# Four modulation loads issued ahead of the small vectors' wait, and TensorE's own quarter moved behind VectorE's three

## The reference

```python
def first_block(x, c, w_ada, b_ada, norm1_w, w_in, ...):
    c_act = jax.nn.silu(c)
    for l in range(DEPTH):                       # DEPTH = 1
        mod = c_act @ w_ada[l] + b_ada[l]        # (1, 1024) @ (1024, 6144)
        sh1, sc1, g1, sh2, sc2, g2 = jnp.split(mod, N_MOD, axis=-1)
        h = modulate(rms_norm(x, norm1_w[l]), sh1, sc1)   # h * (1 + scale) + shift
        mix = hybrid_mixer(h, w_in[l], ...)
        ...
```

## Time and profile before

| what | us |
|---|---|
| median of 3 runs (lowest, highest) | 2472.39 (2470.84, 2477.18) |
| the profiled execution | 2470.67 |
| its span | 2468.9 |
| TensorE busy | 2235.4 (91%) |
| VectorE busy | 1310.5 (53%) |
| ScalarE busy | 879.9 (36%) |
| GpSimd busy | 675.2 (27%) |
| first wide product of `h` starts at | 56.38 |

### The profile page before, as it was taken

One profiled execution on the slowest core, in us unless ns is written; L12 is line 12 of the kernel. 1 busy time (PEld: TensorE's weight loads), 2 busy tenths in 40 slices (PEclk: granted clock), 3 DMA queues, 4 the chain that ended last, 5 costly groups with the idle time before them and its releaser, 6 DMA issues.

```text
span 2468.9 us, 31624 instructions
## 1 busy us (share of the span) xinstructions
PE 2235.4 (91%) x10606; PEld 1829.6 (74%) x10606; DVE 1310.5 (53%) x1758; ACT 879.9 (36%) x1299; POOL 675.2 (27%) x663
## 2 busy tenths in 40 slices
PE   5799999999889989999974999998888886999998
PEld 5688878878768768888863888886666564888886
DVE  6667665676643444333238444433676766544432
ACT  2322322232222233232222554422565654544421
POOL 3278666776740040000222000012032321000021
PEclk6899999999999989999996999999899997999999
DMA  6233333332323323333320333333111120333332
GB/s 213 77 108 100 86 85 98 102 94 85 94 68 94 94 69 94 96 99 89 99 85 17 94 94 94 89 102 89 43 43 60 42 67 19 98 98 93 95 96 64
DMA packets 351923, 211.42 MB, mean 86 GB/s; under 512 B 8648, under 2 KB 339842, under 8 KB 351875
## 3 DMA queue, kind: packets, MB, share of 16 engines
q1 hardware_dynamic: 343130, 184.67, 25.7%
q0 software_dynamic: 7680, 25.17, 3.4%
q10 hardware_dynamic: 1065, 0.96, 0.1%
HBM read 208.67 MB, written 2.10 MB: 85 GB/s over the span
## 4 chain that ended last, share of the span: by engine, by line
PE 72%; DVE 14%; issue 6%; ACT 5%; DMA 1%; POOL 1%; ACTq 0%; DVEq 0%; POOLq 0%; SPq 0%
PE ps L1852 22%; PE ps L1854 21%; PE ps L1853 21%; PE ps L2000 3%; PE ps L1879 2%; ACT at_swap L1020 1%; DVE w_lo L1111 1%; DVE small L1761 1%; DVE small L1440 1%; DVE gd_y_t L1414 1%; DVE gd_q_s L1301 1%; ACT w_hi L698 1%; DVE gd_q_g L1402 1%; PE ps L1949 1%; DMA ada<-w_ada 1%
## 5 line engine op out<-in xcount | busy, mean ns | idle before, releaser
L1852 PE MATMUL ps<-h_hi,w_hi 128*128 128x512 f32 x1896 | 776.8, 410 | 42.0 <-DVE gd_y_t L1414 9.1
L1111 DVE TENSOR_TENSOR w_lo<-raw,w_hi 128x1024 fp32r<-128x1024 f32 x335 | 441.2, 1318 | 602.1 <-ACT w_hi L698 599.6
L1854 PE MATMUL ps<-h_hi,w_lo 128*128 128x512 f32 x1896 | 753.4, 397 | 0.0
L1853 PE MATMUL ps<-h_lo,w_hi 128*128 128x512 f32 x1896 | 752.4, 397 | 0.0
L698 ACT ACTIVATE w_hi<-raw 128x1024 fp32r<-128x1024 f32 x335 | 354.2, 1058 | 731.1 <-PE ps L1854 680.6
L1852 PEld LDWEIGHTS ps<-h_hi,w_hi 128*128 128x128 f32 x1896 | 365.9, 193 | 116.2 <-issue 39.4
L1854 PEld LDWEIGHTS ps<-h_hi,w_lo 128*128 128x128 f32 x1896 | 364.1, 192 | 80.1
L1853 PEld LDWEIGHTS ps<-h_lo,w_hi 128*128 128x128 f32 x1896 | 365.8, 193 | 68.7
L544 POOL TENSOR_TENSOR sq_tmp<-x 128x512 f32 (+1 forms) x40 | 57.5, 1436 | 1061.2 <-DVE x L1612 686.6
L1852 PE MATMUL ps<-act_hi,w_hi 128*128 128x512 f32 x528 | 205.4, 389 | 0.0
L1853 PE MATMUL ps<-act_lo,w_hi 128*128 128x512 f32 x528 | 205.4, 389 | 0.0
(11 more groups left out here) (313 smaller groups left out, 2847.4 us busy)
## 6 DMA issues: line engine op xcount, KB each, us to landing
raw<-ffn_w_up SPq DMA_DIRECT2D x88, 512.0 KB, 3.8
raw<-w_in SPq DMA_DIRECT2D x72, 512.0 KB, 3.8
raw<-w_ffn_in SPq DMA_DIRECT2D x44, 512.0 KB, 3.8
ada_w<-w_ada POOLq DMA_DIRECT2D x64, 256.0 KB, 3.3
raw<-ffn_w_down SPq DMA_DIRECT2D x32, 512.0 KB, 3.6
raw<-diff_w_qkv SPq DMA_DIRECT2D x24, 512.0 KB, 3.7
ada<-w_ada SPq DMA_DIRECT2D x4, 2048.0 KB, 15.3
ada_w<-w_ada_f POOLq DMA_DIRECT2D x32, 256.0 KB, 3.2
```

Source lines behind the costliest of these rows:

```text
L1111: nc.vector.tensor_tensor(w_lo[:, tile.slot], raw[:, tile.raw], w_hi[:, tile.slot].bitcast(F32), SUB)\
L1852: nc.tensor.matmul(dst, w_hi[:, tile.slot, k], hi, start=first, stop=False)
L1853: nc.tensor.matmul(dst, w_hi[:, tile.slot, k], lo, start=False, stop=False)
L1854: return nc.tensor.matmul(dst, w_lo[:, tile.slot, k], hi, start=False, stop=last)
```

## The change

SP no longer waits for the small vectors ahead of the four wide loads, and issues them in the order 0, 2, 3, 1. On TensorE the loop over VectorE's three quarters, with `sums` in it, now stands ahead of the wait for `cact` and quarter 1 and of the 32 matmuls on that quarter; the signal to VectorE hangs on the last of these.

```diff
-            sp.wait_ge(pack_in, 16 * 17)
-            for n in range(4):
+            for n in (0, 2, 3, 1):
                 sp.dma_start(ada0[:, :, T * n:T * n + T], w_ada[:, :, T * n:T * n + T]).then_inc(ada_in[n], 16)
...
             pe.wait_ge(x_odd, 1)
+            for turn_n, q in enumerate((0, 2, 3)):
+                pe.wait_ge(ada0_own, KD * (turn_n + 1))
+                for j in range(4 * q, 4 * q + 4):
+                    nc.tensor.matmul(bank(1)[:, j:j + 1], ada0_sum[:, P * j:P * j + P], one_col, start=True, stop=True)
+                if turn_n == 0:
+                    sums(N_MIX)
+
             pe.wait_ge(pro_dve, 5)
             pe.wait_ge(ada_in[1], 16)
             for j in range(4, 8):
                 for k in range(KD):
-                    nc.tensor.matmul(bank(1)[:, j:j + 1], ada0[:, k, P * j:P * j + P], cact[:, 1, k:k + 1],
-                                     start=k == 0, stop=k == KD - 1)
-
-            for turn_n, q in enumerate((0, 2, 3)):
-                pe.wait_ge(ada0_own, KD * (turn_n + 1))
-                for j in range(4 * q, 4 * q + 4):
-                    s = nc.tensor.matmul(bank(1)[:, j:j + 1], ada0_sum[:, P * j:P * j + P], one_col, start=True, stop=True)
-                if turn_n == 0:
-                    sums(N_MIX)
+                    s = nc.tensor.matmul(bank(1)[:, j:j + 1], ada0[:, k, P * j:P * j + P], cact[:, 1, k:k + 1],
+                                         start=k == 0, stop=k == KD - 1)
             s.then_inc(pro_pe, 1)
             norm(N_MIX)
```

## The result

The changed kernel takes 2480.45 us (median of 14 runs, 2475.26 to 2482.29), the one before 2470.77 us (14 runs beside them, 2465.52 to 2477.18). The forecast was +9.4 us, 0.38%, or 2481.8 us. The profiled execution took 2477.61 us, 6.9 more than the profiled one of before.

A forecast was written before the change was run, and what follows sets the result against it. Bound: completion of the modulation vector. VectorE's last turn ending at 46.0, plus 1.86 and 13.79 on TensorE, gives 61.65 against 52.25, +9.4 us; on the 2472.4 median, 2481.8 us, range 2477 to 2489.

The forecast's parts named there:

- The bound: First 56 us: the rest starts when the modulation vector is complete and the first norm scaled; last group ends at 52.25.
- The loads: SP's wide loads, issued at about 1.9, land at about 17, 22.5, 28 and 33.5; VectorE waits for none.
- VectorE's start: VectorE's first turn starts at 18.28 instead of 21.57, 3.3 us earlier, with zero delay taken for the small vectors.
- VectorE beside GpSimd: GpSimd's six remaining pairs at 3.12 us end at 36.9; VectorE fits 12 operations beside them and ends at 46.0.
- The wait at L1133: VectorE's 3.6 us idle before the mean of the squares, from 40.65 to 44.26, is gone.
- TensorE's order: TensorE's own quarter, 13.79 us at half clock, comes wholly onto the path behind VectorE's last turn: 61.65 against 52.25, +9.4 us.
- Moves as a block: Everything behind the modulation event shifts with it, 0 given back; ±1.5 us kept for the clock's recovery.
- The sign that the prediction set for itself: End of the kernel: the forecast is wrong if the shift at 60 is not there at the end.
- The other sign: TensorE's turns of the small vectors: the forecast is wrong, by A or B, if they start later than 16.2.
- A: Rival: SP's stalled issues hold up ScalarE's small-vector issues, so `cact` and squares come late: +19, 2492 us; chance 0.14.
- B: Rival: wide loads share the DMA engines with `x`, which lands up to 5.4 us late: +14, 2486; chance 0.05.
- C: Rival: TensorE's own quarter runs at full clock, event at 53.8: +1.6 us, 2474; chance 0.06.

The follow-up runs named there:

- SP's part alone: Kernel before with the four wide loads issued without the wait, TensorE's order kept: ratio 0.9989 in order 0, 1, 2, 3; 1.0042 in order 0, 2, 3, 1.
- added wide matmuls: Changed kernel plus four wide float32 matmuls of 512 columns, result unused, in TensorE's idle time between groups of sums; ratio 1.0036 to the kernel before.
- kernel with few squares: Changed kernel with GpSimd's squares for the first norm taken over 16 of 512 columns only; ratio 1.0005 to the kernel before.
- TensorE's part alone: Changed kernel with SP's wait and load order 0, 1, 2, 3 restored, own quarter still last on TensorE; ratio 1.0045 to the kernel before.

## Why the prediction was right, point by point

**The bound.** Right. The time moves with the event that it named, within the intervals, as the table shows over nine kernels.

**The loads.** The direction was right, the times were early. The first quarter lands at 18.65 and not at 17, the second at 24.1 and not at 22.5, the last at 35.2 and not at 33.5 (from the waits of the two kernels with SP's part alone). I had let the transfer begin at 10.5, when the DMA engines fell idle before, and had left out most of the 2.6 us of a landing that are not transfer: 10.5 + 5.4 + 2.6 is 18.5. In the changed kernel VectorE still did not wait for any of them, but only because it started late, as the next point tells; in the same kernel with the added wide matmuls it waited 0.34 us for the first quarter and started at 18.76. So "none is waited for" was wrong by some tenths of a us, and the gain of 3.3 us could not have come whole.

**VectorE's start.** Mis-sized: 19.29 instead of 18.28, a gain of 2.3 and not 3.3 us. The small vectors were turned only 0.23 us later, as the zero for them said; but the short operation L1206 on `cact` took 0.98 us beside GpSimd (0.24 before). It had started 0.07 us after a GpSimd operation (18.06 and 17.99) and ended with it; before, it was over when the next one began at 18.20. This is chance from one trace to the next: of the kernels with the loads early and GpSimd's squares whole, two others met it (1.04 and 0.78 us), three did not (0.18 to 0.29).

**VectorE beside GpSimd.** Mis-sized the other way, by as much. GpSimd was done at 35.42 and not at 36.9, so the last turns ran free sooner; the 3.12 us for a pair, taken from the earlier trace rows, held where VectorE ran its sums (pairs start at 23.37 and 26.48). I had put six such pairs, but the one that starts before 20.52 was all but through when VectorE came, and two more were only partly slowed (2.85 us from 20.52 to 23.37, and 2.7 for the last). The end, 45.89, is the 46.0 of the sum by luck: two errors of 1 us that cancel. The strict form of the Trainium skill's port rule ("SBUF — State Buffer", section "Who interferes with whom"), which would have put VectorE's end at some 50, does not hold here in its size for the long operations; for the short L1206 it does, which ended within 0.02 us of the GpSimd operation it had met. That GpSimd is what slows VectorE is confirmed by the kernel with few squares.

**The wait at L1133.** Right: gone, 3.6 us.

**TensorE's order.** Right, and shown by taking it away: 13.65 us on the path, at the half clock; TensorE's part alone costs 9.8 us in the trace, and leaving out seven eighths of the matmuls gives 11.8 back.

**Moves as a block.** Right within what the times can tell: +9.2 us at the first wide product and 8.6 (7 to 10.6) by the ratio. The sign that the prediction set for itself, that the shift must still be there at the end, holds in the two profiled executions only roughly, and their traces show that the shift is not constant on the way:

| SP's first load of | before | changed | shift |
|---|---|---|---|
| `w_o` | 831.10 | 841.80 | +10.7 |
| `w_ffn_out` | 1134.35 | 1142.69 | +8.3 |
| `ffn_w_down` | 1568.69 | 1579.04 | +10.4 |
| end of the span | 2468.9 | 2475.8 | +6.9 |

Part of this goes with TensorE's clock in stages that the edit does not touch: from the first load of `w_o` to that of `w_ffn_in` (882.93 and 891.99) the kernel before took 51.8 us at a mean granted clock of 0.97, the changed one 50.2 us at 1.00. The clock's rise behind the prologue, for which ±1.5 us was kept, also shifted by less than the event: it came 5.6 us after the first wide product before, and within the window from 69 to 70 (mean granted clock 0.74), some 4 us after it, now. With one trace of each, what is due to the edit and what differs from execution to execution stays open. The other sign, `pack`'s turns later than 16.2, came in by 0.2 us (16.39) without A or B: `x` was there early, and its turns took 5.63 us instead of 5.19, for a reason that no run here shows.

**The rivals.** A did not come: ScalarE's issues were not held up by 18.27 us of stalled issues on SP. B did not come: `x` landed at 10.92. C did not come: the x64 row is 13.79 us long at a granted clock of 0.50. The measured 8.6 stands 1.2 us above the bound of 7.4 set for "slower by over 0.3%", and its interval reaches just below it, as the split of the forecast's chance had allowed.

## What to carry to other kernels

Work that an engine did beside another's is only free at the place where it stood: before moving it behind a wait on that other engine, write down what it was hidden by, since TensorE's 13.8 us cost nothing ahead of VectorE's last turn and all of themselves behind it. An earlier load is worth only as much as the consumer's own path is shorter: here 2.9 us for loads that left 11.6 us sooner, and another 4.5 us once the two things next in line, a wait for a mean and GpSimd's squares, had been moved out of the way as well. And the order of loads has to follow the order of their users: with the own quarter first on TensorE, loading it last cost 11.1 us.

## What the runs showed of the hardware that I had not expected

- TensorE's granted clock fell while the engine was busy without a gap. In the kernel with added wide matmuls it stood at 1.00 from 46 to 48 and fell to 0.50 between 48 and 50, in the midst of the unbroken x64 row (21 rows in 2 us at the full clock, 11 at the half one).
- SP stalled for 18.27 us in issuing four loads of 2 MB, and ScalarE's issues beside it kept to 0.3 to 0.6 us each, as without it.
- A VectorE operation on 128 x 8 elements took 0.98 us instead of 0.24 beside a GpSimd operation on 128 x 512, and GpSimd's root on 128 x 4 elements 1.93 instead of 1.19 beside `w_lo`: the price of this contention lies in the other engine's operation, not in one's own size. In the three traces in which L1206 started after a GpSimd operation (by 0.07, 0.02 and 0.28 us) it ended 0.01 to 0.02 us after that operation's end.
- The DMA writes of the wide loads, at 388 GB/s from 19 to 25 us, did not slow VectorE at all: 0.78 us for each of the seven sums in the first turn of the kernel with few squares, as in the last turn of before.
